# A sixth of the gate matrix stays on chip, and the weighing of gathered words moves behind the first tile's multiply

## The reference, cut to what matters

```python
def chunk(xc):                       # xc: 512 tokens x 1024
    q = (xc @ w_q).reshape(ch, PEER_HEADS, 2, half)
    s = jnp.einsum('thpd,hpnd->thpn', q, sub_keys)
    ...                              # two top-16 lists a head, 256 sums, top 16 of them
    g = jax.nn.softmax(vals, axis=-1)
    u = u_tab[e]                     # e: 128 expert numbers a token
    act = jax.nn.gelu(jnp.einsum('td,thkd->thk', xc, u)) * g
    return jnp.einsum('thk,thkd->td', act, v_tab[e])
x = x + peer(rmsnorm(x, norm_ffn[l]), ...)
```

## Time and profile before

| | us |
|---|---|
| three runs | 3898.29, 3900.83, 3905.68; median 3900.83 |
| the profiled execution | 3911.05, with a span of 3909.2 in the trace |
| `experts` of layer 0 | 1190.6 to about 1800 |
| `experts` of layer 1 | 3300.8 to the end |
| busy over the span | PE 3497.0, DVE 2347.6, ACT 1350.6, POOL 638.7 |

### The profile page before, as it was taken

The page is one execution under the profiler, slowest core; times in us unless marked ns, Lnnn a source line. Parts: engine busy times, 40 slices in busy tenths (PEclk is TensorE's granted clock), DMA queues, the critical chain, the costliest instruction groups (busy, mean ns, idle before and its releaser), DMA issues. The chain is left out here.

```text
span 3909.2 us, 50394 instructions
## 1 busy us (share of the span) xinstructions
PE 3497.0 (89%) x16354; PEld 2799.3 (72%) x16354; DVE 2347.6 (60%) x4877; ACT 1350.6 (35%) x1965; POOL 638.7 (16%) x529
## 2 busy tenths in 40 slices
PE   8779999999996999986674987999999996999998
PEld 6558888788885777774442646888878885777776
DVE  4536766555555777764206634766745553777776
ACT  3433332344442333331012632333334443333332
POOL 0000000000004555550000000000000001555552
PEclk9889999999998999998686998999999998999999
DMA  3113433344538999991110012433334545999997
GB/s 142 43 66 115 147 133 122 132 148 156 198 145 298 318 318 327 316 324 63 61 45 0 2 44 81 145 132 126 134 116 156 196 156 197 326 323 307 327 322 254
DMA packets 317697, 680.65 MB, mean 174 GB/s; under 512 B 33312, under 2 KB 172704, under 8 KB 315680
## 3 DMA queue, kind: packets, MB, share of 16 engines
q1 hardware_dynamic: 270816, 494.73, 36.9%
q0 software_dynamic: 45056, 134.38, 9.9%
q10 hardware_dynamic: 1728, 50.33, 3.1%
HBM read 559.79 MB, written 119.54 MB: 174 GB/s over the span
## 5 line engine op out<-in xcount | busy, mean ns | idle before, releaser
L803 PE MATMUL up_ps<-up_hhi,up_hi 128*128 128x512 f32 x2048 | 810.7, 396 | 7.6 <-PEq L1695 7.6
L1674 POOL DMA_INDIRECT ex_gz<-gelu,ga_atz x256 | 303.1, 1184 | 3135.0 <-POOLq L2027 2738.8
L803 PE MATMUL up_ps<-up_hlo,up_hi 128*128 128x512 f32 x2048 | 799.8, 391 | 0.0
L803 PE MATMUL up_ps<-up_hhi,up_lo 128*128 128x512 f32 x2048 | 799.2, 390 | 0.0
L2186 PE MATMUL ex_psy<-ex_vh,ex_ah 128*128 128x512 f32 x1536 | 615.1, 400 | 134.8 <-DVE ex_al L2250 83.6
L794 DVE TENSOR_TENSOR up_lo<-up_raw,up_hi 128x1024 fp32r<-128x1024 f32 x256 | 313.6, 1226 | 592.3 <-ACT up_hi L790 581.5
L2186 PE MATMUL ex_psy<-ex_vl,ex_ah 128*128 128x512 f32 x1536 | 607.0, 395 | 0.0
L2186 PE MATMUL ex_psy<-ex_vh,ex_al 128*128 128x512 f32 x1536 | 606.1, 395 | 0.0
L811 ACT ACTIVATE up_z<-up_ps 128x512 f32<-128x512 f32 x256 | 153.0, 598 | 902.4 <-PE up_ps L803 902.2
L2186 PEld LDWEIGHTS ex_psy<-ex_vh,ex_ah 128*128 128x128 f32 x1536 | 293.3, 191 | 223.6 <-issue 88.9
L803 PEld LDWEIGHTS up_ps<-up_hhi,up_hi 128*128 128x128 f32 x2048 | 386.6, 189 | 84.8 <-DVE up_lo L794 8.4
(11 more groups left out here) (368 smaller groups left out, 4012.4 us busy)
## 6 DMA issues: line engine op xcount, KB each, us to landing
up_raw<-in_uT SPq DMA_DIRECT2D x256, 512.0 KB, 3.3
ex_vr<-in_v SPq DMA_DIRECT2D x256, 512.0 KB
gelu<-up_z SPq DMA_DIRECT2D x256, 256.0 KB, 2.0
gate_matrix<-sg_gbuf ACTq DMA_DIRECT2D x12, 4096.0 KB, 12.4
ex_gm<-gate_matrix SPq DMA_DIRECT2D x128, 384.0 KB
ex_z<-gelu SPq DMA_DIRECT2D x256, 192.0 KB
ro_wq<-in_peer_wq SPq DMA_DIRECT2D x32, 512.0 KB, 4.4
up_raw<-in_a_w_in SPq DMA_DIRECT2D x14, 512.0 KB, 3.5
```

Source lines behind the costliest of these rows:

```text
L803: last = pe.matmul(self.ps[:, a, :], w[:, a, dc, :], h[:, dc, :], start=(dc == 0 and m == 0), stop=(dc == DC - 1 and m == 2))
L1674: pool.indirect_dma_start(z[:, j:j + 1], None, zmat.rearrange("p k (t a) -> (p k t) a", a=1), bass.IndirectOffsetOnAxis(ap=self.at_z[:, j: ...
```

## The change

Three things. (1) The copies of the odd 64-token blocks go into a new tile `ga_last`, which lives until the layer's v products end; the sixth block is not written to `gate_matrix` and not loaded from it, and the multiply of each tile becomes two, 320 columns from `ex_gm` and 64 columns from `ga_last`. (2) In layer 0 the tile's 32 KB serve `front0` as its scratch `work`. (3) In `experts` the call of `weigh` moves from the head of the iteration behind the multiply of its first tile, in every iteration.

```diff
--- before.py
+++ after.py
@@ -895,7 +895,6 @@
         "scored": A, "maxed": A, "expd": A, "scaled": A, "turn": 2 * A, "stored": 2 * A, "summed": A})
     with ExitStack() as c:
         early = k.sb(c, "f0_early", [P, 2, NL, S])
-        work = k.sb(c, "f0_work", [P, 2, DC, S])
         y = k.sb(c, "f0_y", [P, NL, S])
         gw = k.sb(c, "f0_gw", [P, NL, 2, P])
         prob = k.sb(c, "f0_p", [P, 2, 2, MEMLEN])
@@ -905,6 +904,7 @@
         ps = k.ps(c, "f0_ps", [P, 8, 512])
         block = c.enter_context(nc.Block())
 
+        work = ga.last[:].rearrange("p n t -> p (n t)").rearrange("p (a n t) -> p a n t", a=2, n=DC)
         flat = early[:].rearrange("p a n t -> p (a n t)")
         xn = flat[:, 0:TT * D].rearrange("p (t d) -> p t d", t=TT)
         mxn = flat[:, TT * D:(TT + MT) * D].rearrange("p (t d) -> p t d", t=MT)
@@ -1635,6 +1635,7 @@
         self.at_v = k.sb(c, f"ga_atv{l}", [P, HK], U32)
         self.at_z = k.sb(c, f"ga_atz{l}", [P, HK], U32)
         self.gate = k.sb(c, f"ga_gate{l}", [P, HK])
+        self.last = k.sb(c, f"ga_last{l}", [P, NK, TB])
         self.v_in = [k.sig(f"ga_v{b}") for b in range(NV)]
         self.z_in = [k.sig(f"ga_z{b}") for b in range(NZ)]
         self.counts = {"added": HK, "weighed": HK // 4, "mul": NK, "ah": NK}
@@ -2011,7 +2012,7 @@
     turned.passed(3)
 
 
-def spread_gates(k, l, rows, up, zmat, gmat):
+def spread_gates(k, l, rows, up, ga, zmat, gmat):
 
 
 
@@ -2028,7 +2029,8 @@
         now = k.sb(c, f"sg_now{l}", [P, 2, 3, TB])
         left = k.sb(c, f"sg_left{l}", [P, R, Q, NK])
         right = k.sb(c, f"sg_right{l}", [P, R, Q, NK])
-        gbuf = k.sb(c, f"sg_gbuf{l}", [P, 2, NK, TB])
+        gbuf = k.sb(c, f"sg_gbuf{l}", [P, NK, TB])
+        blocks = (gbuf[:], ga.last[:])
         ps = k.ps(c, f"sg_ps{l}", [P, R, Q, NK])
         block = c.enter_context(nc.Block())
         iota = k.col("iota")
@@ -2088,16 +2090,18 @@
                         act.wait_ge(written[par].sem, i * 16 + written[par].base)
                     for n in range(NQ):
                         act.wait_ge(spread.sem, blk * NQ + spread.done(n))
-                        act.activation(gbuf[:, par, :, n * Q:(n + 1) * Q].rearrange("p i t -> p t i"), ps[:, n % R, :, :],
+                        act.activation(blocks[par][:, :, n * Q:(n + 1) * Q].rearrange("p i t -> p t i"), ps[:, n % R, :, :],
                                        ACT.Copy).then_inc(stored.sem, 1)
                         if n in AFTER:
                             j = par * PT + AFTER[n]
                             up.gelu(act, i * BT + (B0 + j), j % GT)
                             if not (last and j >= BT - GT):
                                 up.high(act, i * BT + (B0 + GT + j), j % GT)
+                    if last and par == 1:
+                        continue
                     act.wait_ge(stored.sem, blk * NQ + stored.done(NQ - 1))
                     act.dma_start(gmat[:, bass.ds(blk, 1), :, :].rearrange("p a i t -> p (a i t)"),
-                                  gbuf[:, par, :, :].rearrange("p i t -> p (i t)")).then_inc(written[par].sem, 16)
+                                  blocks[par].rearrange("p i t -> p (i t)")).then_inc(written[par].sem, 16)
 
             pair(0, first=True)
             with act.Fori(1, NTB // 2 - 1) as i:
@@ -2117,12 +2121,12 @@
             up.keep(sp, zmat, NK - 1, (BT - 1) % GT)
             for s in up.kept:
                 sp.wait_ge(s.sem, s.base + s.credit + 16 * NK // GT)
-            for s in written:
-                sp.wait_ge(s.sem, s.base + 16 * (NTB // 2))
+            for par, s in enumerate(written):
+                sp.wait_ge(s.sem, s.base + 16 * (NTB // 2 - par))
     for s in (staged, spread, stored):
         s.passed(NTB * NQ)
-    for s in written:
-        s.passed(16 * (NTB // 2))
+    for par, s in enumerate(written):
+        s.passed(16 * (NTB // 2 - par))
 
 
 def experts(k, l, x, ga, zmat, gmat):
@@ -2145,7 +2149,7 @@
         vr = k.sb(c, f"ex_vr{l}", [P, GT, D])
         vh = k.sb(c, f"ex_vh{l}", [P, 2, GT, D], F32R)
         vl = k.sb(c, f"ex_vl{l}", [P, 2, GT, D], F32R)
-        gm = k.sb(c, f"ex_gm{l}", [P, 2, NTB, GT, TB])
+        gm = k.sb(c, f"ex_gm{l}", [P, 2, NTB - 1, GT, TB])
         zz = k.sb(c, f"ex_z{l}", [P, 2, GT, SD])
         ah = k.sb(c, f"ex_ah{l}", [P, 2, GT, SD], F32R)
         al = k.sb(c, f"ex_al{l}", [P, 2, GT, SD], F32R)
@@ -2228,7 +2232,6 @@
                 dve.tensor_tensor(w, w, ga.gate[:, bass.ds(i * 4, 4)], ALU.mult).then_inc(s_["weighed"].sem, 1)
 
             def iteration(i, half):
-                weigh(i, half)
                 for par in range(2):
                     g = i * 2 + par
                     for a in range(GT):
@@ -2240,8 +2243,12 @@
                             dve.wait_ge(g_loaded[par].sem, i * 16 + g_loaded[par].base + 16)
                         dve.wait_ge(z_loaded[par][a].sem, i * 16 + z_loaded[par][a].base + 16)
                         blocks = zz[:, par, a, :].rearrange("p (b t) -> p b t", t=TB)
-                        dve.tensor_tensor(blocks, blocks, gm[:, par, :, a, :], ALU.mult).then_inc(s_["mul"].sem, 1)
+                        dve.tensor_tensor(blocks[:, 0:NTB - 1, :], blocks[:, 0:NTB - 1, :], gm[:, par, :, a, :], ALU.mult)
+                        dve.tensor_tensor(blocks[:, NTB - 1:NTB, :], blocks[:, NTB - 1:NTB, :], ga.last[:, bass.ds(g * GT + a, 1), :],
+                                          ALU.mult).then_inc(s_["mul"].sem, 1)
                         b = half * 4 + q
+                        if q == 0:
+                            weigh(i, half)
                         dve.drain()
                         dve.wait_ge(ga.v_in[b].sem, (i - half) * 8 + (ga.v_in[b].base + 16))
                         dve.scalar_tensor_tensor(out=x[:, TD, :], in0=gv[:, b, :], scalar=gz[:, bass.ds(i * 4 + q, 1)],
@@ -2295,7 +2302,7 @@
             up.ps = k.ps(c, f"up_ps{l}", [P, GT, 512])
             route(k, l, up, self.wq, self.wq_loaded, zmat, vals, key1, key2)
             gate_softmax(k, l, vals, key1, key2, rows, up, ga, zmat)
-            spread_gates(k, l, rows, up, zmat, gmat)
+            spread_gates(k, l, rows, up, ga, zmat, gmat)
             up.finished()
 
 
@@ -2305,7 +2312,7 @@
         k.dram = dram
         k.params = k.sb(ctx, "params_sb", [P, NCOLS])
         x = k.sb(ctx, "x_sb", [P, TT, D])
-        gmat = nc.dram_tensor("gate_matrix", (P, NTB, NK, TB), F32, kind="Internal").ap()
+        gmat = nc.dram_tensor("gate_matrix", (P, NTB - 1, NK, TB), F32, kind="Internal").ap()
         zmat = nc.dram_tensor("gelu", (P, NK, S), F32, kind="Internal").ap()
         kv = [(k.sb(ctx, f"ma_kT{l}", [P, MEM_CH, MEMLEN]), k.sb(ctx, f"ma_v{l}", [P, MT, 2 * P])) for l in range(LAYERS)]
 
```

## The result

The changed kernel takes 4020.32 us in the median of four runs (4007.96 to 4030.24), the kernel before, run beside it, 3903.26 (3898.29 to 3917.9). The ratio is 1.0292, with a 95% interval of 1.0246 to 1.0338: 117 us lost where 50 were forecast, and above the range's 4010. The profiled execution took 4011.69 us with a span of 4009.9, so the two profiled executions stand 101 us apart.

What follows compares the result with a forecast made beforehand. The prediction took the loop from DVE's weighing through POOL's gathers to the second scaled addition as the bound. The moved weighing's 70 us less 19.6 from the dropped write gave +50 us, 3951 on the runs' median; range 3885 to 4010.

Steps and rivals of the forecast that it cites:

- What bounds the kernel: V products: a loop from DVE's weighing through POOL's gathers to the second scaled addition, 18.2 us an iteration.
- The dropped write: Start of the v products: without the block write they begin earlier, 19.6 us gained over both layers.
- The smaller loads: Gate loads fall by a sixth, 128 KB an iteration: 0.42 us of 18.2 if transfers set the interval.
- the split multiply: DVE's part of the loop: one more instruction a tile, 0.1 us each, 0.4 an iteration, uncovered.
- The moved weighing: Loop of the v products: gathers issued later, interval 19.4 instead of 18.2, 70 us over 58 intervals.
- weighing to second scaled addition: First term of the loop's sum, taken as 7.6 us, between 7.34 and 9.73, with less loaded transfers.
- the rest of the interval: Other loop terms: to the old weighing's place 8.8, v tile wait 0.8, low and multiply 1.8, split multiplies 0.4.
- the landings give it back: Rival, chance 0.17: first term and v tile wait total 7.2 us, not 8.4; 3881, or 3855 if transfers set the interval.
- Worse than forecast: Rival, chance 0.17: landings don't ease, first term 8.4, v tile wait 1.5, interval 20.9; 4038 us.
- the wait for the v tile: DVE's wait before an iteration's first low: 0.8 us in the forecast, 1.5 in the worse rival.
- PE's clock: In the worse rival: clock at 0.50 after PE's pauses, 1.7 us an iteration, hidden at the forecast's interval.
- The signs: First gate load 2.2 us behind last gelu write, interval 19.4, gathered-row wait some 100 us, low wait down, transfer share 0.87.

Runs made afterwards that it cites:

- e2: Kernel before with only the weighing moved behind the first multiply: 4047.6 us, 1.0382.
- e4: Changed kernel with POOL's four v gathers of an iteration put ahead of its four word gathers, weighing still late: 3878.1 us, 0.9939.
- e11: Kernel before with only POOL's order altered, v gathers ahead of word gathers: 3832.7 us, 0.9821.
- e10: e1 with room in memory for six blocks a partition, the sixth neither written nor read: 3859.7 us, 0.9884.
- e7: e1 with the sixth block's write and its wait put back, and six blocks' room in memory: 3882.4 us, 0.9957.
- e1: Changed kernel with the weighing back at the iteration's head, so the block on chip alone: 3878.6 us, 0.9934.
- e6: Changed kernel with the first scaled addition of each iteration over 128 of its 1024 columns: one execution of 4000.6 us.
- e3: Changed kernel with the weighing between the first low and the first multiply, 0.7 us earlier: 3929.4 us, 1.0082.
- e14: Changed kernel with room in memory for six blocks, the sixth unused: 4024.4 us, 1.0298.
- e13: Changed kernel with weighing at the head, v gathers first and issued early at stage start, six blocks' room in memory: 3821.7 us, 0.9798.

## Why the prediction was wrong in size and right in kind

**What bounds the kernel.** Right. The loop from the weighing through POOL's queue to the second scaled addition was tight, and e2 and e4 show it from both sides: lengthening it costs 145 us, opening it in the changed kernel gives 142 (4020 to 3878), of which 55 are there without the move too. e11 shows that the kernel before lost 73 us to it already. DVE's waits for gathered rows come to some 100 us over its two layers (layer 1 in the earlier trace rows), and in e11 9 us are left, all before the first addition of a layer.

**The dropped write.** 19.6 us forecast, 18 in the trace, 23 between e10 and e7. Right.

**The smaller loads and the split multiply.** The two multiplies took 483 and 217 ns where one took 552 (125 of each in layer 1), but they overlap: from the start of the first to the end of the last it is 0.62 us, so the second adds 0.07 us a tile where I took 0.1. What the smaller loads gave back was not measured by itself: behind the border's 18 us, e1's 24 leave 6 for both together and e10's 46 leave 28.

**The moved weighing.** The step that failed is the first term of the sum round the loop, "weighing to second scaled addition", which I put at 7.6 us. Measured over 58 iterations of the changed kernel (weighing to second scaled addition of iterations 1 to 29 of each layer, mean of the differences of their starts) it is 8.53. In the kernel before, the same mean is 8.50, and the earlier trace rows, the two iterations that I went by, lie on either side of it. So I counted on a fall by 0.9 us from lighter loaded transfers, and in sum there was none. The way from the v gather's issue to its use did shorten, from 6.67 to 5.86 us (7.02 in the 33 of 58 iterations in which DVE waited for the rows). But the issue came later behind the weighing, 2.67 us where it was 1.82; the 1.67 of my reading was an iteration in which DVE stood idle beside POOL's word gather. In the new place it hardly ever does, because the scaled addition follows at once: the word gather takes 1.90 us in the mean where it took 1.04. The prediction had no term for that. e6 shows that it is the addition's doing; what it is worth in time lies between the 0.39 us an iteration that e6 shows at the second scaled addition and the whole 0.85, and no run parts it further, since e3 moves the weighing as well.

The other terms hold: the rest of the interval came to 11.8 in my sum (8.8 + 0.8 + 1.8 + 0.4), and over the same 58 iterations to 20.07 - 8.53 = 11.5. The mis-sized term is 0.93 x 58 = 54 us, and 50 + 54 = 104 is near what the profiled pair shows (101). That this comes out so close is partly luck: the 0.2 us that the rest was too long is made up for by the interval before, which I put at 18.2 and which is 18.0 over these 58, and by the first and last intervals of each layer, which grew too. The median's 117 lies above the pair's 101 because the profiled run of the changed kernel lies 9 us below its median and that of the kernel before 8 us above.

**The rivals.** The way from issue to use eased by 0.8 us, about the part that I had built in; the further 1.2 us that "the landings give it back" needed did not come. "Worse than forecast" came nearest in time, 4038, and its first term, 8.4, is nearly the measured 8.53. But it put that down to landings that don't ease, and they did; the late issue made up for it. Nor did its other parts hold: the wait for the v tile didn't grow (1.5 assumed there, 0.94 found between the last al and the first low, where it was 1.54 before), and PE's clock didn't decide. PE's pauses and the lower clock did appear, 0.91 to 0.97 in the plateaus, and they lay beneath the loop: e4, without any edit to PE, has its clock at 1.00 from 3400 to 3800 again.

**The signs.** All pointed the right way: the first gate load 2.5 us behind the end of the last gelu write's issue, the interval up (20.2 for 19.4), DVE's wait for gathered rows up at q = 1 (138.5 for about 100), the wait before lows down (53.4 from 69.4), the transfers' share down (0.81 to 0.84 for 0.87).

## What to carry to other kernels

An instruction that releases a queue can be worth more than its own length: before moving it, list everything that stands behind the released wait, and which of it the same iteration needs. Here 0.15 us of DVE work, moved by 1.8 us, cost 145 us, and swapping two loops on POOL, so that nothing needed soon stood behind that wait, gave 73. When an issue is moved, read its length in the neighbourhood where it will run, not in the one where it ran.

## What was not expected of the hardware

An indirect gather's issue on POOL takes 0.94 us when DVE is idle, and up to 2.0 when it starts inside one of DVE's instructions on two tensors: in the kernel before 0.94 in the mean for the 198 issues that started while DVE ran nothing, 1.54 for the 135 that started inside a scaled addition (sorted by their times in the trace). Those 135 ended 0.78 us behind the end of the addition, in the mean, as if most of the issue began only then. At the weighing it took 1.93 us beside an addition over 1024 columns and 0.99 beside one over 128. DVE's instruction is not lengthened in turn: the 151 additions that started inside an issue took 1.285 us in the mean, the 93 that met none 1.285. The Trainium skill, "SBUF — State Buffer", section "SBUF: two separate sides", has DVE and GpSimd take one pair of ports in turn for whole instructions, and names instructions of DVE with two operands in SBUF among those that take it, against a GpSimd operation that reads SBUF. The runs agree where DVE is first, with 1.93 and 0.99. That the one that starts first keeps the ports, whichever it is, they don't show for POOL, with the 1.285 on either side; whether a gather's issue holds the ports for its whole length is not known.

The same loads from a tensor laid out for six blocks instead of five ran 19 us faster in one kernel, and not in two others (e10, e14, e13).
